# Rotary angles moved from a block's first norm to the end of its gated attention, and 32 modulation dots given other times

## What is computed

```python
cos, sin = rope_tables(positions)          # positions times 32 frequencies, cosine and sine
for l in range(DEPTH):
    mod = cond @ w_ada[l] + b_ada[l]       # 6 x 1024 modulation values
    h = rms_norm(x) * (1.0 + scale_a) + shift_a
    proj = h @ w_in[l]
    ...
    log_a = jax.nn.log_sigmoid(g_a @ w_gate_up + b_gate) / GLA_TAU
    o = gla_chunked(q, k, v, log_a)                        # gated linear attention
    o = rms_norm(o, gla_out_norm) * jax.nn.silu(g_o)
    q_nope = rms_norm(q_nope); q_pe = apply_rope(rms_norm(q_pe), cos, sin)
    k_nope = rms_norm(k_nope); k_pe = apply_rope(rms_norm(k_pe), cos, sin)
    mla_out = mla_attention(q_nope, q_pe, k_nope, k_pe, mv)  # causal softmax attention
    x = x + gate_a * (concat(o, mla_out) @ w_out[l])
    ...                                    # MLP, with the second half of mod
```

## Time and profile before

| | us |
|---|---|
| median of 3 runs | 4149.39 (4148.74 to 4149.45) |
| profiled execution | 4143.9 |
| its span | 4141.7 |
| PE busy | 4029.7 |
| DVE busy | 2215.8 |
| ACT busy | 1476.3 |

### The profile page before, as it was taken

How to read it: one execution, slowest core, us unless ns; L and a number is a source line. 1 busy time by engine, 2 the same in 40 slices (tenths; PEclk the granted TensorE clock), 3 DMA queues, 4 the chain that set the end, 5 groups by cost and what they waited for, 6 DMA issues and landing times.

```text
span 4141.7 us, 47445 instructions
## 1 busy us (share of the span) xinstructions
PE 4029.7 (97%) x18830; PEld 3085.5 (74%) x18830; DVE 2215.8 (53%) x3450; ACT 1476.3 (36%) x2416; POOL 102.4 (2%) x162
## 2 busy tenths in 40 slices
PE   8999999999999999999999999999999999999997
PEld 5677656888888877665788888877777777887785
DVE  7777565634344566466633333554445363646756
ACT  4433554412122333545422121343434343225533
POOL 2000000000000000000000000000000000000000
PEclk9999999999999999999999999999999999999998
DMA  6533201233332220200122211231111111116541
GB/s 234 191 97 121 81 6 31 67 100 99 92 107 87 83 86 26 89 16 16 51 82 77 78 60 46 69 115 44 44 41 44 44 46 62 45 58 224 183 168 56
DMA packets 97461, 337.93 MB, mean 82 GB/s; under 512 B 10776, under 2 KB 11832, under 8 KB 96090
## 3 DMA queue, kind: packets, MB, share of 16 engines
q1 hardware_dynamic: 77514, 258.87, 18.9%
q0 software_dynamic: 19728, 76.03, 5.9%
HBM read 300.25 MB, written 34.60 MB: 81 GB/s over the span
## 4 chain that ended last, share of the span: by engine, by line
PE 83%; DVE 10%; ACT 3%; issue 2%; DMA 1%; SPq 0%; DVEq 0%; POOL 0%; ACTq 0%
PE PS L1300 34%; PE PS L1282 19%; PE PS L2369 4%; PE PS L2234 3%; PE PS L3432 2%; PE PS L3495 2%; PE PS L1682 1%; PE PS L1265 1%; PE PS L2826 1%; PE PS L1961 1%; PE PS L1955 1%; PE PS L2853 1%; PE PS L2147 1%; PE PS L2839 1%; PE PS L3199 1%
## 5 line engine op out<-in xcount | busy, mean ns | idle before, releaser
L638 ACT ACTIVATE WH<-raw 128x1024 fp32r<-128x1024 f32 x314 | 330.5, 1053 | 686.7 <-PE PS L1300 454.1
L1282 PE MATMUL PS<-hi,WH 128*128 128x512 f32 x1248 | 525.5, 421 | 1.5 <-ACT vf L1390 1.1
L1300 PE MATMUL PS<-hi,WH 128*128 128x512 f32 x1312 | 513.4, 391 | 3.3 <-DVE lo L1139 2.2
L1300 PE MATMUL PS<-lo,WH 128*128 128x512 f32 x1312 | 515.3, 393 | 0.0
L1300 PE MATMUL PS<-hi,WL 128*128 128x512 f32 x1312 | 513.9, 392 | 0.0
L1282 PE MATMUL PS<-hi,WL 128*128 128x512 f32 x1248 | 492.0, 394 | 0.0
L1282 PE MATMUL PS<-lo,WH 128*128 128x512 f32 x1248 | 489.2, 392 | 0.0
L649 DVE TENSOR_TENSOR WL<-raw,WH 128x1024 fp32r<-128x1024 f32 x274 | 334.9, 1222 | 136.2 <-ACT WH L638 136.0
L1300 PE MATMUL PS<-al,WH 128*128 128x512 f32 x768 | 301.8, 393 | 0.0
L1300 PE MATMUL PS<-ah,WL 128*128 128x512 f32 x768 | 300.3, 391 | 0.0
L1300 PE MATMUL PS<-ah,WH 128*128 128x512 f32 x768 | 299.9, 391 | 0.0
(11 more groups left out here) (478 smaller groups left out, 6976.1 us busy)
## 6 DMA issues: line engine op xcount, KB each, us to landing
adab<-in_w_ada POOLq DMA_DIRECT2D x120, 512.0 KB, 4.6
raw<-in_win SPq DMA_DIRECT2D x104, 512.0 KB, 3.6
raw<-in_down SPq DMA_DIRECT2D x80, 512.0 KB, 3.6
raw<-in_up SPq DMA_DIRECT2D x64, 512.0 KB, 3.6
raw<-in_dft SPq DMA_DIRECT2D x24, 512.0 KB, 3.7
sp_x<-X SPq DMA_DIRECT2D x24, 512.0 KB, 5.7
X<-sp_x SPq DMA_DIRECT2D x24, 512.0 KB, 5.3
raw<-in_wout SPq DMA_DIRECT2D x24, 512.0 KB, 3.7
```

The source lines that it names most:

```text
L638: act.activation(PLACES[PLACE[j]][0], raw[:, j % 2, :], ACT.Copy).then_inc(*W_HI.next(j))
L1282: mm = pe.matmul(bank[b + hf], w[:, k, :], r[:, k, HALF[hf]], start=k == 0 and w is wh and r is hi, stop=k == 7 and w is wl)
L1300: mm = pe.matmul(bank[b + hf], w[:, k, :], r[:, k, HALF[hf]], start=k == 0 and w is wh and r is hi, stop=k == 7 and w is wl)
```

## The change

Four things are changed, all in layer 0.

- The 32 dots get other ticks: 11 at 24 to 62 (3.8 apart), 11 at 72 to 89 (1.7 apart), 10 at 115 to 150 (3.9 apart).
- The rotary angles are computed at `gla_at(0, 0) + 157` and later, behind the last dot, instead of in the norm. Their buffers are the halves of the two slots `adab`.
- The two halves share these buffers. The second half's positions are loaded after the first half's angles are done, and each of its results waits for the store of the first half's.
- The norm units that use the slots as scratch wait for the stores or the last angle instead of the last dot. The wait of the value copies for the stores is gone.

```diff
-    q += [(0, j, gla_at(0, 0) + 20 + 5.4 * (j - 16)) for j in range(16, 48)]
+    free = [24 + 3.8 * i for i in range(11)] + [72 + 1.7 * i for i in range(11)] + [115 + 3.9 * i for i in range(10)]
+    q += [(0, 16 + i, gla_at(0, 0) + at) for i, at in enumerate(free)]
...
-                self.rang, self.rk = flat[:, S:S + HS], flat[:, S + HS:2 * S]
-                self.rr = self.VT[:, 4:8, :]
+                self.rang, self.rk = self.adab[:, 0, HS:S], self.adab[:, 1, HS:S]
+                self.rr = [self.adab[:, x, 0:HS] for x in range(2)]
...
-                    if l == 0 and vh + q4 == 0:
-                        dve.wait_ge(*RO_OUT[1])
...
-        def rope_at(hf):
-            return norm_at(0, 0) + 26 + 8 * hf
+        def rope_at(hf, x=0):
+            return gla_at(0, 0) + 157 + 8 * hf + 4 * x
...
             for hf in range(2):
-                yield rope_at(hf) + 9
+                yield rope_at(hf) - 2
+                sp.wait_ge(*(RO_DVE["angle", 0, 1] if hf else ADA_DOT[47]))
+                sp.dma_start(m.rang.bitcast(I32), D["pos"][HALF[hf]].partition_broadcast(P)).then_inc(*POS_IN[hf].next(0, by=16))
                 for x in range(2):
+                    yield rope_at(hf, x) + 5
                     sp.wait_ge(*RO_ACT[hf, x])
-                    sp.dma_start(D["sp_rope"][x][:, HALF[hf]], m.rr[:, 2 * hf + x, :]).then_inc(*RO_OUT.next(hf, by=16))
+                    sp.dma_start(D["sp_rope"][x][:, HALF[hf]], m.rr[x]).then_inc(*RO_OUT[x].next(hf, by=16))
...
                 for x in range(2):
-                    yield rope_at(hf) + 4 * x
-                    r = m.rr[:, 2 * hf + x, :]
-                    reduce_angle(dve, DVE_OWN, m.rang, m.rk, r, x == 1)
+                    yield rope_at(hf, x) + 0.2
+                    if hf:
+                        dve.wait_ge(*RO_OUT[x][0])
+                    reduce_angle(dve, DVE_OWN, m.rang, m.rk, m.rr[x], x == 1)
...
-                    yield rope_at(hf) + 4 * x + 3.5
+                    yield rope_at(hf, x) + 4.2
                     act.wait_ge(*RO_DVE["angle", hf, x])
...
                     elif u.rows == 64:
                         act.wait_ge(*GL_PE["gate", l, 1, 1])
-                        act.wait_ge(*ADA_DOT[95 if l else 47])
+                        act.wait_ge(*(ADA_DOT[95] if l else RO_DVE["angle", 1, 1]))
                     else:
                         act.wait_ge(*WI_ACT["evac", l, 1 if lane % 2 else 3, 1])
-                        act.wait_ge(*ADA_DOT[95 if l else 47])
+                        act.wait_ge(*(ADA_DOT[95] if l else RO_OUT[1][1]))
+                        if l == 0:
+                            act.wait_ge(*RO_OUT[0][1])
```

More of the change, by code:

```diff
@@ L533, in build @@
         POS_IN = [signal("pos_loaded_0"), signal("pos_loaded_1")]
-        RO_DVE, RO_ACT, RO_OUT = signal("rope_dve"), signal("rope_act"), signal("rope_stored")
+        RO_DVE, RO_ACT = signal("rope_dve"), signal("rope_act")
+        RO_OUT = [signal("rope_sine_stored"), signal("rope_cosine_stored")]
         GL_PE, GL_ACT, GL_DVE = signal("gla_pe"), signal("gla_act"), signal("gla_dve")
@@ L1431, in rope_dve @@
                 dve.wait_ge(*POS_IN[hf][0])
[L1432 to L1436 removed]
+                dve.tensor_copy(m.rk, m.rang.bitcast(I32)).then_inc(*DVE_OWN.next())
+                dve.wait_ge(*DVE_OWN.now())
+                dve.tensor_scalar(m.rang, m.rk, vc("invf"), None, ALU.mult).then_inc(*DVE_OWN.next())
                 dve.wait_ge(*DVE_OWN.now())
                 for x in range(2):
[L1439 to L1441 removed]
+                    yield rope_at(hf, x) + 0.2
+                    if hf:
+                        dve.wait_ge(*RO_OUT[x][0])
+                    reduce_angle(dve, DVE_OWN, m.rang, m.rk, m.rr[x], x == 1)
                     dve.wait_ge(*DVE_OWN.now())
[L1443 removed]
+                    dve.tensor_scalar(m.rr[x], m.rr[x], -PI, None, ALU.max).then_inc(*RO_DVE.next("angle", hf, x))
         def rope_act(act):
@@ L1447, in rope_act @@
                 for x in range(2):
-                    yield rope_at(hf) + 4 * x + 3.5
+                    yield rope_at(hf, x) + 4.2
                     act.wait_ge(*RO_DVE["angle", hf, x])
-                    act.activation(m.rr[:, 2 * hf + x, :], m.rr[:, 2 * hf + x, :], ACT.Sin, bias=0.0).then_inc(
-                        *RO_ACT.next(hf, x))
+                    act.activation(m.rr[x], m.rr[x], ACT.Sin, bias=0.0).then_inc(*RO_ACT.next(hf, x))
         LA, E1, BB, DD = (X[:, 4 + i, :] for i in range(4))
@@ L1936, in mla_sp @@
             if l == 0:
-                sp.wait_ge(*RO_OUT[1])
+                for x in range(2):
+                    sp.wait_ge(*RO_OUT[x][1])
             for x in range(2):
```

12 lines of the change are left out of this document (removed).

## The result

| | before | after |
|---|---|---|
| median of the runs | 4149.07 us (4146.9 to 4149.45, 4 runs) | 4231.45 us (4226.09 to 4234.05, 4 runs) |
| ratio | | 1.0201, 95% interval 1.0189 to 1.0214 |
| profiled execution, span | 4143.9, 4141.7 us | 4229.5, 4227.5 us |
| mean granted clock | 0.994 | 0.985 |
| ACT busy, instructions in the profile | 1476.3 us | 1555.8 us |

The account below looks back on a forecast made before the run. PE, busy 4029.7 of 4141.7 us, was taken as the bound. Terms -6.5 + 6.5 - 4 - 1.5 + 5.3 + 22.7 + 26 = +48.5 us gave 4192.4 profiled, forecast 4197.9 with the runs' median 5.5 higher; range 4168 to 4230.

Parts of the forecast that it names:

- angles out of the norm: Gap at 212 to 224 us: DVE's gate work starts up to 4.7 us earlier and the clock stays up; -6.5 us.
- dots, 11 in a row: Between the pairs: two slots refill too slowly for 11 dots, delaying the decayed keys' product that PE awaits; +6.5 us.
- dots off the chains: Behind the row, until the second pair's first level ends: dots leave chain steps, PE's 3.71 us wait shrinks; -4 us.
- second pair's later levels: Levels after the second pair's first: about as many dots as before, at better places; -1.5 us.
- angles at the end of the gated attention: Near 395 to 424 us: the second half's late positions and Sin delay ACT's squares, for which PE waits; +5.3 us.
- loads in gates and first units: 419 to 520 us: alternating Exp and Ln table loads make ACT late, 11 of 18 us idle time used; +22.7 us.
- loads in the attention steps: 536 to 658 us: 28 loads, 24 of them delaying PE by their length less some slack; +26 us.
- the four hidden ones: Attention steps: loads that fit into ACT's existing 1.28 us wait for PE's sum, which occurs 4 times.
- a drain of about 1.38 us: Rival: every table load costs twice its length, adding about 60 us; 4258 us, chance 0.03.
- the two rivals of the attention steps: Steps hide their loads, 4172 us, chance 0.15; or PE's clock falls in them, 4218 us, chance 0.15.
- rival of the clock: Attention steps: PE's clock at the lower level for 40 of some 190 us adds 20; 4218 us, chance 0.15.

Follow-up runs that it names:

- one copy: Kernel before, with one plain 128x512 copy on ScalarE at each of 28 places in the first layer's attention steps, no load added: 4164.44 us, ratio 1.0044.
- the kernel with the loads alone: Kernel before, with only the Sin table set loaded where the changed kernel has its last Sin, so later Ln and Exp bring their own tables: 4226.89 us.
- the dots alone: Kernel before, with only the new places of the 32 modulation dots, angles still in the norm and no table load added: 4158.87 us, ratio 1.0025.
- early and late loads: Changed kernel; early: alternating loads kept only in gates and first units, 4186.01 us; late: kept only in the attention steps, 4201.32 us.
- two (36.0 us): Kernel before, with two plain 128x512 copies on ScalarE at each of 28 places in the first layer's attention steps, no load added: 4192.55 us, ratio 1.0105.
- With three: Kernel before, with three plain 128x512 copies on ScalarE at each of 28 places in the first layer's attention steps: 4219.58 us, ratio 1.0173.
- the set loaded again: Changed kernel, with the table set holding both Exp and Ln loaded again right behind the last Sin: 4153.96 us, ratio 1.0015.

## Why the prediction was wrong, point by point

By the shifts of the two profiled executions:

| step | forecast | range given | measured | of it slower or faster matmuls |
|---|---|---|---|---|
| angles out of the norm | -6.5 | -7.7 to -4.7 | -5.8 | -2.9 |
| dots, 11 in a row | +6.5 | 0 to 11 | +9.0 | +3.8 |
| dots off the chains | -4 | -5.7 to -2.3 | -4.8 | -2.9 |
| second pair's later levels | -1.5 | -3 to 0 | +0.7 | 0 |
| angles at the end of the gated attention | +5.3 | 2 to 8 | +5.5 (6.4 without the loads) | see next row |
| loads in gates and first units | +22.7 | 12 to 32 | +29.9 | +12.0 with the row above |
| loads in the attention steps | +26 | 13 to 31 | +43.7 | +18.4 |
| behind the first layer | 0 | | +5.9 | +5.9 |
| sum, with +1.7 ahead of the change | +48.5 | | +85.8 | |

The last column is how much longer the same instructions of PE are busy; the rest of a step is time in which PE stands. One cause runs through the larger misses: the forecast priced how long PE stands, and put the fall of TensorE's clock behind it at nothing.

**Wrong: the attention steps.** This is the step that failed, by 17.7 us. The term of +26 is 30.8 us of loads in the open less 4.8 us of slack, and PE does stand 25.3 us more. What the term left out is the clock: 18.4 us of slower matmuls. The prediction had this as a rival, with +20 for 40 us at the lower level, and gave it 0.15. It was that rival which happened: a mean clock of 0.90 over 186.8 us is 37 us at the lower level. The reason for the low chance was the argument that slower matmuls would be partly covered by PE's waiting. At most a small share was: PE stands 25.3 us more where 30.8 us of loads lie in the open, so 5.5 us were caught by slack and by slower matmuls together. The two can't be told apart here; with one copy, at full clock, slack alone caught 2.5 of 17.5 us.

The weighing is what should have been different. The profile of before showed the clock fall twice in this stage, each time behind gaps in which PE was busy about half or less of some microseconds, and the forecast itself put gaps of that kind into each of 14 steps. A clock that had fallen at both gaps seen was no one-in-seven case.

**Short: gates and first units.** +29.9 instead of +22.7, inside its range; 28.5 and 30.8 in two experiments, a tail of 6.4 taken off in the first, which has the angles there. ACT is busy 17.9 to 18.9 of 20 us from 440 to 500 us, a little under the 95% that were foreseen. What the term left out is again the clock: it stands at 0.78 to 0.95 from 420 to 520 us, and in the kernel with the loads alone PE stands 20.6 us more, near the forecast, with 10.2 us of slower matmuls on top. The estimate that 11 of 18 us of idle time would be used wasn't tested by itself.

**Right: the loads' count and length**, 73 in all, 1.283 us, and the four hidden ones. By the Trainium skill ("ScalarE: Activation LUTs", section "What ACT_TABLE_LOAD costs") each would also have brought a drain of about 1.38 us, and the time would have been 4258 by the prediction's estimate. No row shows such a gap (0.5 us of idle time before 26 loads), and the loads ahead of the square made PE's wait longer by their length and 0.14 us. What the section "Table sets: the hidden batching unit" on the same page of the Trainium skill says, to group activations by set, holds here with a measured price: 77.5 us for one missing preload.

**Right: the norm**, -5.8, half standing and half clock, with the clock steady at both old gaps; and **the angles' tail**, with its cause: SyncE's queue behind the Sins. The positions' load, estimated at 2 to 5 us, took 3.2.

**Wrong in size: the dots.** The three terms gave +1; both traces give +4.9, the median of the dots alone +10.8. The delay of the decayed keys' product was forecast well, 6.6 us against 6.5, although the row that it rests on was misread: the 0.28 us at 311.01 are time that PE already stood, not time to spare. What the row cost beyond is the clock, 2.4 us behind the product and 1.6 at 288 us. The first is the case for which the prediction set its upper bound of 11: the clock falls there in all six kernels with the row of 11 and in none of the others. The second also comes in three kernels with the old dots (290 to 294 us), and its cause isn't known.

The last term had the wrong sign. The shift rises by 1.0 between 384 and 398 us, and the lists of DVE show why: between the decays (L1584, L1577 after) and the keys (L1594, L1587 after) of this level stands one dot before, at 387.53, and two after, at 383.09 and 388.47. PE's wait for the keys grows by the length of one dot (first fence before, second after, DVE and then PE):

```profile
387.53 1.25 DVE L688 CUSTOM_DVE_ANT_0 adab<-adab,cond 128x1024 f32<-128x1024 f32 x1
...
390.06 1.11 PE L1682 MATMUL PS<-X 64*128 64x64 f32 x16 [0.56 <-DVE X L1594]
```

```profile
383.09 1.22 DVE L690 CUSTOM_DVE_ANT_0 adab<-adab,cond 128x1024 f32<-128x1024 f32 x1
...
388.47 1.25 DVE L690 CUSTOM_DVE_ANT_0 adab<-adab,cond 128x1024 f32<-128x1024 f32 x1
...
391.20 1.11 PE L1675 MATMUL PS<-X 64*128 64x64 f32 x16 [1.89 <-DVE X L1587]
```

In the kernels with early and late loads the clock falls there too, and the rise is 4.3 and 4.0 us. No experiment moved this dot alone.

**The range.** "The terms' ends alone give from +16 to +74" is a wrong sum: the ends as stated give +11 to +75. The range of 4168 to 4230 was set by the two rivals of the attention steps and hangs on it only in part.

**Behind the first layer** nothing was expected and nothing is changed, and the 5.9 us are falls of the clock; see the last section. The prediction's rival of the clock, 4218 us, was nearest to the measured 4231.45. By the shifts it lacks the rest of the gates (7.2 us), these last steps (5.9) and the rest of the dots (3.9).

## What to carry to other kernels

Moving one activation function past a table preload can cost far more than the work moved: list ScalarE's table loads of both versions before anything else, and put the common set back behind the stranger. When work is put in front of something that TensorE waits for, price it at its length only if the gaps stay as short as those the kernel already has; where the profile shows the clock falling behind a gap, take the clock's cost into the forecast and not into a rival. And where a load is queued behind a store that waits for a late engine, issue it first: one changed order on SyncE gave 6 to 7 us here.

## What the runs showed of the hardware

**Twice the delay, well over twice the price.** One copy at each of 28 places (17.5 us) cost 15.0 us by the trace and 17.0 by the median, with the clock at 1.00; two (36.0 us) cost 50.8 and 44.2 with the clock at 0.83. With three the clock hardly falls further (0.81).

**A table load delays others by its length** and no more that shows: 1.283 us, the next activation 0.01 us behind it, and two of them made PE's wait 2.71 us longer. Plain copies of the same length, 5 us more of them in the open, cost 44.2 us where the loads cost 47.3; that the two are worth the same to the microsecond isn't shown.

**The clock also falls where nothing is changed.** In the changed kernel three steps of 1.6 to 1.7 us in the shift stand in the stretch from 1595 to 1998 us (by the times of before). One of them in the windows view, and the same work in the kernel before:

```profile
1640.00:1660.00 20.00, 20.00 (x98) 14.06 (x98) 9.46 (x15) 5.79 (x7) 0.00 (x0) 0.92 0.09 27
```

```profile
1560.00:1580.00 20.00, 20.00 (x106) 14.06 (x104) 9.45 (x17) 5.79 (x7) 0.00 (x0) 1.00 0.08 27
```

0.08 of 20 us is 1.6 us, with PE busy throughout and the other engines busy alike. The kernel with the loads alone has the falls at 1640 and 1700 us too, that with the set loaded again has none. Such steps, here and ahead of 420 us, are a likely source of the spread of 12 us among ten runs of one kernel (4148.6 to 4160.4), and a reason why differences of 2 us can't be read from two traces; that they are its source was not tested.
